# Feed-forward convolution sums in the idle accumulator banks, with the first tap and the halo copies on ScalarE

## What is computed

```python
def causal_dwconv(u, w):           # w: (taps, channels), per channel, causal
    ...
def conv_ffn(h, w_up, w_conv, w_down):
    u = causal_dwconv(h @ w_up, w_conv)        # 1024 -> 2 * 2816 channels, 3 taps
    gate, val = jnp.split(u, 2, axis=-1)
    return (jax.nn.silu(gate) * val) @ w_down  # 2816 -> 1024

    h = rms_norm(x, ffn_pre_norm[l])
    y = conv_ffn(h, ffn_w_up[l], ffn_conv_w[l], ffn_w_down[l])
    x = x + rms_norm(y, ffn_post_norm[l])
```

## Time and profile before

| | |
|---|---|
| Median of 3 runs | 2615.87 us (2614.61 to 2616.7) |
| Profiled execution, first to last instruction (span) | 2608.6 us |
| TensorE matmuls busy | 2532.9 us, 97% |
| VectorE busy | 1534.2 us, 59% |
| ScalarE busy | 919.9 us, 35% |
| GpSimd busy | 841.4 us, 32% |
| TensorE's granted clock over the span | 0.995 |

### The profile page before, as it was taken

How to read it: one execution, slowest core, us unless ns; L and a number is a source line. 1 busy time by engine, 2 the same in 40 slices (tenths; PEclk the granted TensorE clock), 3 DMA queues, 4 the chain that set the end, 5 groups by cost and what they waited for, 6 DMA issues and landing times.

```text
span 2608.6 us, 32631 instructions
## 1 busy us (share of the span) xinstructions
PE 2532.9 (97%) x11713; PEld 2102.9 (81%) x11713; DVE 1534.2 (59%) x2448; ACT 919.9 (35%) x1519; POOL 841.4 (32%) x346
## 2 busy tenths in 40 slices
PE   8999999999999999999999999999999999999997
PEld 7877788888787888887888887888887888878886
DVE  4798867887644533458346287255386264682462
ACT  6433232222344333333333343334334233332332
POOL 6531100000032000044544444444345444445342
PEclk9999999999999999999999999999999999999999
DMA  8895675856777767743532335333335332334331
GB/s 257 284 352 215 216 292 187 305 180 226 267 290 286 283 229 262 255 133 96 179 89 92 99 117 170 105 89 97 98 114 181 94 92 87 105 113 154 89 97 65
DMA packets 313816, 452.62 MB, mean 174 GB/s; under 512 B 12072, under 2 KB 234557, under 8 KB 292669
## 3 DMA queue, kind: packets, MB, share of 16 engines
q1 hardware_dynamic: 305101, 438.56, 49.6%
q10 hardware_dynamic: 8560, 12.06, 1.3%
HBM read 368.78 MB, written 81.79 MB: 173 GB/s over the span
## 4 chain that ended last, share of the span: by engine, by line
PE 90%; DVE 5%; issue 1%; DMA 1%; ACT 1%; SPq 0%; ACTq 0%; DVEq 0%
PE colb L1554 19%; PE colb L1556 18%; PE colb L1555 18%; PE accb L1554 11%; PE accb L1556 11%; PE accb L1555 11%; PE colb L1591 2%; DVE accb L1246 2%; PE accb L1766 1%; DMA raw<-in_xattn_wq 1%; DMA kept<-pair 0%; ACT junk L700 0%; DVE small L1086 0%; DVE small L1087 0%; DVE xh L1093 0%
## 5 line engine op out<-in xcount | busy, mean ns | idle before, releaser
L647 POOL TENSOR_TENSOR pair<-raw,pair 128x1024 fp32r<-128x1024 f32 x339 | 840.5, 2495 | 1739.6 <-ACT pair L679 1729.1
L1554 PE MATMUL colb<-hT,pair 128*128 128x512 f32 x1952 | 764.0, 391 | 17.0 <-issue 14.0
L1556 PE MATMUL colb<-hT,pair 128*128 128x512 f32 x1952 | 760.5, 390 | 0.0
L1555 PE MATMUL colb<-hT,pair 128*128 128x512 f32 x1952 | 760.4, 390 | 0.0
L679 ACT ACTIVATE pair<-raw 128x1024 fp32r<-128x1024 f32 x339 | 355.5, 1053 | 482.5 <-PE accb L1556 277.6
L1554 PE MATMUL accb<-pair,act 128*128 128x512 f32 x1120 | 439.2, 392 | 12.2 <-issue 4.6
L1554 PEld LDWEIGHTS colb<-hT,pair 128*128 128x128 f32 x1952 | 367.0, 188 | 102.1 <-issue 27.1
L1556 PE MATMUL accb<-pair,act 128*128 128x512 f32 x1120 | 436.6, 390 | 0.0
L1555 PE MATMUL accb<-pair,act 128*128 128x512 f32 x1120 | 436.6, 390 | 0.0
L1556 PEld LDWEIGHTS colb<-hT,pair 128*128 128x128 f32 x1952 | 367.0, 188 | 77.1
L1555 PEld LDWEIGHTS colb<-hT,pair 128*128 128x128 f32 x1952 | 367.1, 188 | 74.9
(11 more groups left out here) (164 smaller groups left out, 2416.7 us busy)
## 6 DMA issues: line engine op xcount, KB each, us to landing
pair<-kept SPq DMA_DIRECT2D x123, 1024.0 KB, 4.9
raw<-in_ffn_w_up SPq DMA_DIRECT2D x176, 512.0 KB, 3.8
raw<-in_ffn_w_down SPq DMA_DIRECT2D x176, 256.0 KB, 3.0
kept<-pair SPq DMA_DIRECT2D x41, 1024.0 KB, 8.4
raw<-in_w_in SPq DMA_DIRECT2D x17, 512.0 KB, 8.4
xh<-in_x SPq DMA_DIRECT2D x4, 2048.0 KB, 13.9
xt<-in_x SPq DMA_DIRECT2D x4, 2048.0 KB, 15.6
x_mixed<-xt SPq DMA_DIRECT2D x4, 2048.0 KB, 11.1
```

The costliest lines, as they stand in the source:

```text
L647: nc.gpsimd.tensor_tensor(pair[:, b, 1, :], raw[:, r, :], pair[:, b, 0, :].bitcast(F32), ALU.subtract).then_inc(lo_done, 1)
L1554: nc.tensor.matmul(dst, sh, mh, start=first, stop=False)
L1555: nc.tensor.matmul(dst, sh, ml, start=False, stop=False)
L1556: return nc.tensor.matmul(dst, sl, mh, start=False, stop=last)
```

## The change

- The convolution sums of pairs 0 to 9 of a half lie in accumulator banks: banks 0 and 1 for even pairs, 2 and 3 for odd ones (`conv_at`). The eleventh pair stays in `cv`.
- The first tap is made by ScalarE, as a copy of the column bank with a scale per channel; it follows the plain copy to `uf`, and the column bank is set free after it. For the first two pairs of a half ScalarE first waits until the accumulator bank is free.
- The halo copies in and out go from VectorE to ScalarE. At a tile's first pair ScalarE waits for the last convolution of the tile before (at the first tile: for the halo's zeroing).
- VectorE keeps two taps each for gate and value. `conv_ready` is set by the last of them.
- TensorE waits for the low parts of ten pairs ahead of the first row slot, and for all eleven ahead of the sixth, in place of two, four, six, eight, ten and eleven ahead of the first six.

```diff
+        def conv_at(j, e):
+
+            return accb[2 * (j % 2) + e][:, :] if j < GF - 1 else cv[:, e, :]
...
                         n = q * GF + j
+                        u = uf[:, j % 2, :, :]
+                        hs = halo.rearrange("p (g f) h -> p g f h", g=2)[:, :, n, :]
+                        if n == 0:
+                            sc.wait_ge(conv_ready, pairs.at(FFN, t, 0) + 1)
+                        nc.scalar.activation(u[:, :, 0:HS], hs, ACT.Copy)
                         for e in range(2):
...
                             hi(FFN, t, i + AHEAD)
                             slot_full(sc, FFN, t, i)
-                            nc.scalar.activation(uf[:, j % 2, e, HS:LS], colb[bank_of(FFN, c)][:, :], ACT.Copy)\
-                                .then_inc(col_free[bank_of(FFN, c)], 1)
+                            nc.scalar.activation(u[:, e, HS:LS], colb[b][:, :], ACT.Copy)
+                            if j < 2:
+                                sc.wait_ge(acc_free[2 * j + e], acc.at(FFN, t, 2 * q) + 1)
+                            nc.scalar.activation(conv_at(j, e), colb[b][:, :], ACT.Copy, scale=par[:, w:w + 1])\
+                                .then_inc(col_free[b], 1)
                         sc.wait_ge(conv_ready, pairs.at(FFN, t, 1 + n) + 1)
-                        nc.scalar.activation(cv[:, 0, :], cv[:, 0, :], ACT.Silu).then_inc(silu_done, 1)
+                        nc.scalar.activation(cv[:, 0, :], conv_at(j, 0), ACT.Silu).then_inc(silu_done, 1)
+                        nc.scalar.activation(hs, u[:, :, T:LS], ACT.Copy)
                         sc.wait_ge(y_ready, ys.at(FFN, t, n) + 1)
-                        nc.scalar.activation(act[:, 0, j, :], cv[:, 1, :], ACT.Copy).then_inc(hi_written, 1)
+                        nc.scalar.activation(act[:, 0, j, :], conv_at(j, 1), ACT.Copy).then_inc(hi_written, 1)
...
-                step(nc.vector.tensor_copy(u[:, :, 0:HS], hs))
                 freed(FFN, t, q * 2 * GF + 2 * j)
                 freed(FFN, t, q * 2 * GF + 2 * j + 1)
-                settle()
-                for k in (2, 0, 1):
+                for k in range(2):
                     for e in range(2):
...
-                        if k == 2:
-                            step(nc.vector.tensor_scalar(cv[:, e, :], u[:, e, k:k + T], w, None, ALU.mult))
...
+                        tap = nc.vector.scalar_tensor_tensor(conv_at(j, e), u[:, e, k:k + T], par[:, at_w:at_w + 1], conv_at(j, e),
+                                                             ALU.mult, ALU.add)
...
-                settle()
-                nc.vector.tensor_copy(hs, u[:, :, T:LS]).then_inc(conv_ready, 1)
                 ve.wait_ge(silu_done, pairs.at(FFN, t, n) + 1)
-                nc.vector.tensor_tensor(cv[:, 1, :], cv[:, 1, :], cv[:, 0, :], ALU.mult).then_inc(y_ready, 1)
+                nc.vector.tensor_tensor(conv_at(j, 1), conv_at(j, 1), cv[:, 0, :], ALU.mult).then_inc(y_ready, 1)
...
-                        if n < (GF + 1) // 2:
-                            pe.wait_ge(lo_written, los.at(FFN, t, q * GF + min(2 * n + 2, GF)))
+                        if n == 0:
+
+                            pe.wait_ge(lo_written, los.at(FFN, t, q * GF + GF - 1))
+                        elif n == GF // 2:
+                            pe.wait_ge(lo_written, los.at(FFN, t, q * GF + GF))
```

More of the change, by code:

```diff
@@ L1001, in ffn @@
                             c = q * 2 * GF + 2 * j + e
+                            b = bank_of(FFN, c)
+                            w = par_at["ffn2"] + n + KF * e
                             hi(FFN, t, i + AHEAD)
                             slot_full(sc, FFN, t, i)
-                            nc.scalar.activation(uf[:, j % 2, e, HS:LS], colb[bank_of(FFN, c)][:, :], ACT.Copy)\
-                                .then_inc(col_free[bank_of(FFN, c)], 1)
+                            nc.scalar.activation(u[:, e, HS:LS], colb[b][:, :], ACT.Copy)
[3 more added lines that the diff above has]
+                                .then_inc(col_free[b], 1)
                         sc.wait_ge(conv_ready, pairs.at(FFN, t, 1 + n) + 1)
-                        nc.scalar.activation(cv[:, 0, :], cv[:, 0, :], ACT.Silu).then_inc(silu_done, 1)
+                        nc.scalar.activation(cv[:, 0, :], conv_at(j, 0), ACT.Silu).then_inc(silu_done, 1)
+                        nc.scalar.activation(hs, u[:, :, T:LS], ACT.Copy)
                         sc.wait_ge(y_ready, ys.at(FFN, t, n) + 1)
-                        nc.scalar.activation(act[:, 0, j, :], cv[:, 1, :], ACT.Copy).then_inc(hi_written, 1)
+                        nc.scalar.activation(act[:, 0, j, :], conv_at(j, 1), ACT.Copy).then_inc(hi_written, 1)
                     for i in range(GF):
@@ L1387, in ffn_pair @@
                 q, j = divmod(n, GF)
-                f = GF * q + j
                 u = uf[:, j % 2, :, :]
-                hs = halo.rearrange("p (g f) h -> p g f h", g=2)[:, :, f, :]
-                step(nc.vector.tensor_copy(u[:, :, 0:HS], hs))
                 freed(FFN, t, q * 2 * GF + 2 * j)
                 freed(FFN, t, q * 2 * GF + 2 * j + 1)
-                settle()
-                for k in (2, 0, 1):
+                for k in range(2):
                     for e in range(2):
-                        base = par_at["ffn2"] if k == 2 else par_at["ffn01"] + k * 2 * KF
-                        w = par[:, base + f + KF * e:base + f + KF * e + 1]
-                        if k == 2:
-                            step(nc.vector.tensor_scalar(cv[:, e, :], u[:, e, k:k + T], w, None, ALU.mult))
-                        else:
-                            settle(1)
-                            step(nc.vector.scalar_tensor_tensor(cv[:, e, :], u[:, e, k:k + T], w, cv[:, e, :],
-                                                                ALU.mult, ALU.add))
-                settle()
-                nc.vector.tensor_copy(hs, u[:, :, T:LS]).then_inc(conv_ready, 1)
+                        at_w = par_at["ffn01"] + k * 2 * KF + n + KF * e
+                        if k:
+                            settle(1)
+                        tap = nc.vector.scalar_tensor_tensor(conv_at(j, e), u[:, e, k:k + T], par[:, at_w:at_w + 1], conv_at(j, e),
+                                                             ALU.mult, ALU.add)
+                        if (k, e) == (1, 1):
+                            tap.then_inc(conv_ready, 1)
+                        else:
+                            step(tap)
                 ve.wait_ge(silu_done, pairs.at(FFN, t, n) + 1)
-                nc.vector.tensor_tensor(cv[:, 1, :], cv[:, 1, :], cv[:, 0, :], ALU.mult).then_inc(y_ready, 1)
-                lo_y(FFN, t, n, act[:, 1, j, :], act[:, 0, j, :], cv[:, 1, :])
+                nc.vector.tensor_tensor(conv_at(j, 1), conv_at(j, 1), cv[:, 0, :], ALU.mult).then_inc(y_ready, 1)
+                lo_y(FFN, t, n, act[:, 1, j, :], act[:, 0, j, :], conv_at(j, 1))
             def attn(p, t):
@@ L1825, in _ @@
             ffn(NT - 1)
-STEPS_PAIR = 7
-STEPS_PREP, STEPS_MIX, STEPS_MIX_LAST, STEPS_ATTN, STEPS_FFN = 159, 180, 82, 45, 183
+STEPS_PAIR = 3
+STEPS_PREP, STEPS_MIX, STEPS_MIX_LAST, STEPS_ATTN, STEPS_FFN = 159, 180, 82, 45, 95
 _INS = ["x", "mem", "mem_norm", "mix_pre_norm", "mix_post_norm", "w_in", "pool_maps", "pool_scale",
```

## The result

| | before | changed |
|---|---|---|
| First comparison, median | 2615.86 us (2614.61 to 2616.70, 4 runs) | 2591.40 us (2587.23 to 2596.01, 4 runs) |
| Ratio, 95% interval | | 0.9912 [0.9896, 0.9927] |
| Second comparison, median | 2612.34 us (16 runs, 2608.48 to 2618.94) | 2591.81 us (2585.81 to 2594.57, 6 runs) |
| Ratio, 95% interval | | 0.9916 [0.9902, 0.9930] |
| Span of the profiled execution | 2608.6 us | 2584.6 us |

(One execution of before, of 12322 us, is left out of the second row.) The change makes the kernel 0.9% faster.

The account below looks back on a forecast made before the run. It took a VectorE-ScalarE loop of 12.06 us per pair against TensorE's 10.88 to stall first halves. Span 2608.6 - 18.8 = 2589.8 us, 2597.1 for the median with 7.3 around the span; range 2593 to 2602.

Parts of the forecast that it names:

- What bounds it, and why the stall is there: First-half column stretches: a VectorE-ScalarE loop of 12.06 us per pair outlasts TensorE's 10.88, until the weights' lead is used up.
- Why the second halves had no stall: Second-half column stretches: without a row pass (1.22 us) the loop is 10.84 us, about TensorE's pace.
- The main term: Four first-half column stretches: their whole excess over the second-half ones goes, 18.8 us.
- The row stretches: TensorE's row slots: 0.83 us each, 3.3 us at most over four; taken as 0, with 3.3 kept for the lower end.
- 7.3 us more, which lies around the span: Outside the profiled span: median 2615.87 us less span 2608.6 us, added to the forecast span to give the forecast median.
- Part by part: Changed VectorE-ScalarE loop priced step by step from neighbouring rows: 9.2 us per pair, under 10.88.
- the new wait: TensorE's first row slot of each half, now needing ten pairs' low parts: 4.0 us to spare, price 0.
- Rival (2): Slow taps into banks delay TensorE's first row slot; kernel slower beyond 2.2 us more per pair, 2634 at 2.39; chance 0.03.
- The rule on the shared port pair: VectorE with two SBUF inputs or in two-port mode takes turns with GpSimd; taps into accumulator banks are free of it.

Follow-up runs that it names:

- three spare operations: Changed kernel with three spare multiply-adds per pair on VectorE ahead of Silu, into an unused buffer: 2621.27 us, ratio 1.0034.
- the last variant: Changed kernel with sums in two SBUF buffers, TensorE's old waits and three spare multiply-adds per pair on VectorE: 2729.55 us, ratio 1.0446.

## Why the prediction missed

- **What bounds it, and why the stall is there: right.** The loop of VectorE and ScalarE, at 12.06 us against 10.88. Every variant that brought it under 10.88 has stretches of 119.7 to 119.8.
- **Why the second halves had no stall: wrong.** The prediction took off the row pass and had the loop at 10.84 us, TensorE's pace. In the trace of before, the Silus of the second halves come 11.15 to 11.39 us apart, here 11.16, and ScalarE waits for VectorE each time:

```profile
1773.84 0.63 ACT L1007 ACTIVATE arena<-arena 128x512 f32<-128x512 f32 x1 [6.27 <-DVE arena L1407]
1785.00 0.63 ACT L1007 ACTIVATE arena<-arena 128x512 f32<-128x512 f32 x1 [6.27 <-DVE arena L1407]
```

The loop was too long there as well; over the ten periods its excess is 3.7 us, and the lead of about 5 us covers it.
- **The main term, 18.8 us: right.** 125.17 + 124.55 + 124.40 + 123.42 became 119.68 + 119.76 + 119.78 + 119.68, 18.6 us.
- **The row stretches, "I take 0 and keep 3.3 for the lower end": a mis-sized term.** They gave 0.6 to 0.7 us each, 2.5 in all. In the trace of before, the starts after a first half lose about 0.3 us once in every pair of slots until the fourth row slot: the tail of the same stall, whose pairs without a row pass still ran at 11.2 us. I had read the cause for these 0.8 us and should have taken most of them.
- **"7.3 us more, which lies around the span": wrong, and the step that put the time out of the range.** Only 1.8 to 3.6 us lie around the span in any of the executions whose span is known. The rest was that the profiled execution was quicker than the three timed. The sum's 2589.8 us for the span with about 2 us around it is 2591.8, against the 2591.4 measured; with 7.3 it became 2597.1. How near 2591.8 comes is luck in part: the span of the changed kernel's trace was 2584.6 us, 5.2 less than the sum's (2.5 of it the row stretches, 2.0 an earlier start of the feed-forward part), and its execution the quickest of four. Executions of before spread from 2605 to 2619 and of the changed kernel from 2586 to 2596, so medians of three or four wander by some us: 2615.9 here, 2612.3 of sixteen. My range had no term for that spread at all. Taken the other way, from 2615.87, the columns and the row stretches (18.6 + 2.5 us) lead to 2594.8, inside the range; no run shows where the other 3.4 us of the first comparison's gain lie.
- **The gain in the feed-forward part itself** is 22.0 us between the first trace of each kernel and 21.3 between the second, and both comparisons hold it within their intervals. Between the first two, 0.9 us of it lie at the starts of two tiles, where a column came 0.65 and 0.86 us after the last row-slot matmul before and 0.32 and 0.34 after. That is spread and not the change: in the second traces it was 0.35 and 0.24 before, 0.51 and 0.52 after.
- **Part by part, the durations: close.** ScalarE's scaled copy into a bank 0.66 us (taken 0.68), small copies 0.20 (0.19), taps 0.75 each and 2.73 for four (2.9), loop 8.9 (9.2), to spare at the new wait 4.1 us (4.0: the tenth pair's low part comes 6.7 us after the copy of its second column begins).
- **What the prediction did not see: that the parts do not add up.** It took the halo copy's 2.35 and the first taps' 2.98 as two costs. Both hold waits for GpSimd, and a wait moves: without the copy, the first taps took over 0.8 us of it, and without the first taps the copy's wait was hidden behind ScalarE. So the first taps alone gave the whole gain, and the halo copies alone most of it.
- **Rival (2), the new wait, has its place right.** It put the point of no gain at 2.2 us more per pair and 2634 at 2.4; with 2.35 us more the kernel took 2621, slower than before (ratio 1.0034). By its formula TensorE would be 4.2 us late in each half at 2.35; it was 2.2. Its price for more (2823 at 4.8) was not tried.
- **The rule on the shared port pair** (the Trainium skill, "SBUF — State Buffer", "Who interferes with whom") agrees with the traces that test it: taps with both inputs in SBUF wait for GpSimd where its subtraction runs already (3.63 and 4.16 us for four), taps with one input in a bank never do (320 between 747 and 757 ns).

```profile
L1411 DVE SCALAR_TENSOR_TENSOR accb<-arena,par,accb x320: 747/750/757, 1135.4 to 2503.0; 128x512 f32<-128x512 f32 x160
```

## What to carry to other kernels

Where the bounding engine pauses at a steady period that is not its own, look for a closed loop of the others: if its period is under that engine's, it costs nothing, and if it is over, it costs the excess times the pairs less the lead that the buffers give. So a cut brings its full worth at first, and nothing more once the lead covers what is left. A long duration of a tiny operation is a wait; taking the operation away may only hand the wait to the next one. And read the span and the time of the same execution, over more than three of them, before you set a range a few microseconds wide.

## What the chip showed beyond that

A pause of TensorE can cost more than itself. After one pause ahead of a row slot (three spare operations; the first row-slot matmul comes 2.43 us after the matmul before), the granted clock of TensorE was (windows as above)

```profile
1616.00:1619.00 3.00, 0.96 (x4) 0.94 0.88 322
1619.00:1621.00 2.00, 2.00 (x6) 0.50 1.03 420
1621.00:1625.00 4.00, 4.00 (x17) 0.87 0.61 201
1625.00:1630.00 5.00, 5.00 (x24) 1.00 0.27 95
```

that is the lower of its two levels, 1.2 GHz, for some 3 us: matmuls started 0.43 us apart and not 0.23, and the stretch of row slots took 61.55 us in place of 59.84. But the length of the pause does not decide it. Of the eight such pauses of this trace, 2.15 to 2.51 us from start to start, four were followed by such a drop, at about 1.7 us each, and four were not, those of 2.46 and 2.44 us among them:

```profile
1250.00:1256.00 6.00, 5.32 (x23) 1.00 0.80 302
1432.00:1438.00 6.00, 5.47 (x24) 1.00 0.26 89
1618.00:1624.00 6.00, 5.35 (x17) 0.72 0.85 324
```

In the last variant a pause of 2.40 us in the columns was followed by a drop, and six of 2.60 to 2.69 us in the first tile were not. Of the pauses of the kernel before, 1.3 us, none was (clock 1.00 in the earlier trace rows). What decides between pauses of like length is not shown.
